# Expert products as plain fp32 in four column groups of the array, on weights that are not split

## What is computed

```python
def expert_choice_ffn(h, w_router, w_gate, w_up, w_down):
    t = h.reshape(bsz * seq, d)
    cap = CAPACITY_FACTOR * n_tok // N_EXPERTS
    probs = jax.nn.softmax(t.astype(jnp.float32) @ w_router.astype(jnp.float32), axis=-1)
    aff, idx = lax.top_k(probs.T, cap)
    xe = t[idx]
    hid = jax.nn.silu(jnp.einsum("ecd,edf->ecf", xe, w_gate)) * jnp.einsum("ecd,edf->ecf", xe, w_up)
    ye = jnp.einsum("ecf,efd->ecd", hid, w_down) * aff[..., None].astype(h.dtype)
    out = jnp.zeros_like(t).at[idx.reshape(-1)].add(ye.reshape(-1, d))
```

## Time and profile before

| | us |
|---|---|
| median of 3 runs | 2584.41 (2583.43 to 2584.87) |
| the profiled execution, its own time | 2584.44 |
| its span in the trace | 2582.5 |
| TensorE busy | 2542.2 |
| VectorE busy | 2194.6 |
| ScalarE busy | 1543.3 |
| first product of the experts starts | 1053.57 |
| last product starts | 2564.90 |

### The profile page before, as it was taken

One profiled execution on the slowest core, in us unless ns is written; L12 is line 12 of the kernel. 1 busy time (PEld: TensorE's weight loads), 2 busy tenths in 40 slices (PEclk: granted clock), 3 DMA queues, 4 the chain that ended last, 5 costly groups with the idle time before them and its releaser, 6 DMA issues.

```text
span 2582.5 us, 34113 instructions
## 1 busy us (share of the span) xinstructions
PE 2542.2 (98%) x13271; PEld 1978.6 (77%) x13271; DVE 2194.6 (85%) x2470; ACT 1543.3 (60%) x1781; POOL 349.4 (14%) x419
## 2 busy tenths in 40 slices
PE   9899999999999999999999999999999999999997
PEld 9788899989988888676767767767667677667765
DVE  6989888988887344899999999999999999999997
ACT  5344444444435122577777777777777777777775
POOL 0322332233321000100000000000000000000002
PEclk9899999999999999899999999999999999999999
DMA  4233223422347343999999999999999999999996
GB/s 174 65 107 125 95 95 104 132 95 95 132 135 261 134 149 119 390 392 378 373 374 378 382 367 384 372 378 370 378 381 374 371 382 371 377 378 371 373 379 244
DMA packets 72303, 705.99 MB, mean 273 GB/s; under 512 B 9840, under 2 KB 14064, under 8 KB 49616
## 3 DMA queue, kind: packets, MB, share of 16 engines
q1 hardware_dynamic: 49232, 628.92, 62.8%
q0 software_dynamic: 14272, 56.60, 7.1%
q10 hardware_dynamic: 8640, 18.29, 1.9%
HBM read 669.72 MB, written 34.06 MB: 273 GB/s over the span
## 4 chain that ended last, share of the span: by engine, by line
PE 95%; DVE 2%; DMA 1%; issue 1%; ACT 1%; POOL 0%; ACTq 0%; DVEq 0%; POOLq 0%
PE p_gu L2462 38%; PE p_y L2493 19%; PE pp L1087 17%; PE pp L1295 5%; PE pp L1131 5%; PE pp L1324 2%; PE pdg L1182 2%; PE p_h L2474 1%; PE off_banks L1165 1%; PE ptr L1149 1%; PE pp L1405 1%; DMA h<-rows 1%; PE off_banks L1179 1%; PE off_banks L1177 1%; PE ptr L1341 0%
## 5 line engine op out<-in xcount | busy, mean ns | idle before, releaser
L2344 DVE TENSOR_TENSOR wl<-raw,wh 128x2048 fp32r<-128x2048 f32 x528 | 1194.2, 2290 | 116.7 <-ACT wh L2241 106.4
L2241 ACT ACTIVATE wh<-raw 128x2048 fp32r<-128x2048 f32 x528 | 990.8, 1911 | 230.5 <-PE p_y L2493 223.1
L2462 PE MATMUL p_gu<-wh,xh 128*96 128x512 f32 x1408 | 566.4, 402 | 1.6 <-DVE xl L2358 1.5
L2462 PE MATMUL p_gu<-wh,xl 128*96 128x512 f32 x1408 | 555.7, 395 | 0.0
L2462 PE MATMUL p_gu<-wl,xh 128*96 128x512 f32 x1408 | 553.7, 393 | 0.0
L2462 PEld LDWEIGHTS p_gu<-wl,xh 128*96 128x96 f32 x1408 | 227.5, 162 | 100.2 <-issue 0.3
L2462 PEld LDWEIGHTS p_gu<-wh,xh 128*96 128x96 f32 x1408 | 227.6, 162 | 90.6 <-DVE wl L2344 2.3
L1087 PE MATMUL pp<-h_hi,wx_hi 128*128 128x256 f32 (+1 forms) x832 | 296.0, 356 | 0.5 <-ACT fo L673 0.5
L2462 PEld LDWEIGHTS p_gu<-wh,xl 128*96 128x96 f32 x1408 | 227.5, 162 | 83.3 <-issue 0.2
L1087 PE MATMUL pp<-h_hi,wx_lo 128*128 128x256 f32 (+1 forms) x832 | 282.7, 340 | 0.0
L1087 PE MATMUL pp<-h_lo,wx_hi 128*128 128x256 f32 (+1 forms) x832 | 281.6, 339 | 0.0
(11 more groups left out here) (283 smaller groups left out, 3798.0 us busy)
## 6 DMA issues: line engine op xcount, KB each, us to landing
raw<-in_w_e SPq DMA_DIRECT2D x176, 3072.0 KB, 10.9
w_raw<-in_w_x SPq DMA_DIRECT2D x48, 512.0 KB, 3.5
dec<-acs POOLq DMA_DIRECT2D x48, 512.0 KB, 4.8
w_raw<-in_w_g SPq DMA_DIRECT2D x24, 512.0 KB, 3.5
g_tab<-gx POOLq DMA_DIRECT2D x8, 1152.0 KB, 6.0
w_raw<-in_w_s SPq DMA_DIRECT2D x16, 512.0 KB, 3.8
gx<-fo ACTq DMA_DIRECT2D x16, 384.0 KB, 3.1
ys<-yt ACTq DMA_DIRECT2D x14, 384.0 KB, 2.7
```

The lines of the kernel that those rows point to most:

```text
L2241: act.activation(wh[:, n % 2, at:at + hi - lo], raw[:, n % RAW, lo:hi], ACT.Copy).then_inc(s_wh, 1)
L2344: dve.tensor_tensor(wl[:, n % 2, to], raw[:, n % RAW, lo:hi], wh[:, n % 2, to].bitcast(F32), ALU.subtract).then_inc(s_wl, 1)
L2462: mm = pe.matmul(p_gu[n % 2][0:SLOTS, 0:w], xx[:, side, k * SLOTS:(k + 1) * SLOTS], ww[:, n % 2, k * w:(k + 1) * w], start=(k == 0 and i = ...
```

## The change

- **No split.** `wh`, `wl`, `xl`, `hid_lo` and the instructions that write them are gone. TensorE multiplies the raw fp32 weights with fp32 tokens.
- **Column groups.** The 96 tokens are three groups of 32. A job is one group of tokens by one tile of 128 hidden columns: 8 products of 256 columns (gate and up) with a 128 x 32 stationary operand. There are 3 x 22 x 16 = 1056 jobs. Four of them make a round, one in each quarter of the array's columns, with the result on partitions 0, 32, 64 and 96 of `p_gu`. There are 264 rounds, and every three rounds finish four tiles.
- **Down.** For each tile, the first 768 columns of the result go as 2 x 3 products of 384 columns to partitions 0 to 95 of `p_y`, and the last 256 as 3 products to partition 96, in `p_y` and in a new bank `p_z`.
- **Transposes.** Each round has one `turn` of 128 x 128 on the whole array, between the two halves of the next round's `gate_up`.
- **ScalarE and VectorE** keep the silu, on 128 x 128, the copies of the turned hidden values and tokens, and the results.
- **Loads.** `raw` has seven slots, and a load waits for `down` of the unit seven before. Unit 0 is asked for where it was. Units 1 and 2 are asked for after GpSimd has issued the prompt's gather, 3 and 4 after the mixer's stores have landed, 5 and 6 after `chosen`.
- **The end.** Squares and norms lie one per round in the last six rounds.

The core of the diff (of functions that are replaced as a whole, mostly the new lines):

```diff
-UNITS = (2,) * 11
-NU = len(UNITS)
-RAW = 3
-UT = max(UNITS)
-TURN_AT = 5
-UW = UT * P * (2 * KD + KD)
+UT = 2
+NU = FT // UT
+EARLY_RAW = 3
+RAW = 7
+TW = P * (2 * KD + KD)
+UW = UT * TW
+QUADS = 4
+GROUPS = SLOTS // 32
+JOBS = GROUPS * FT * E
+ROUNDS = JOBS // QUADS
+HELD = 4
...
                     sp.wait_ge(s_o, NT)
                     load_unit(sp, A, e_raw, s_eraw, 0, 0)
-                    load_unit(sp, A, e_raw, s_eraw, 0, 1)
                 sp.wait_ge(s_h, t + 1)
                 sp.dma_start(h2[t * P:(t + 1) * P, 0:D], hh[:, t % 2, :]).then_inc(s_h2[t % 2], 16)
             sp.wait_ge(s_pr, 2)
             sp.dma_start(probs_of(NTP, NT), prob[:, NTP:NT]).then_inc(m_pr2, 16)
-            load_unit(sp, A, e_raw, s_eraw, 0, 2)
...
-        wh = a.sb("wh", [P, 2, UW], F32R)
-        wl = a.sb("wl", [P, 2, UW], F32R)
+        more = a.sb("more", [P, RAW - EARLY_RAW, UW])
+        raw = [*raw, more[:, 2], more[:, 3], more[:, 0], more[:, 1]]
...
-        hl = a.sb("hid_lo", [P, 2, UT * SLOTS], F32R)
+        xT = a.sb("xT", [P, 2, KD * SLOTS])
+        a.sb("lists", [P, KD * SLOTS * 2])
+        tg = a.sb("tg", [P, 2, P])
+        hid = a.sb("hid", [P, 2, P])
+        hT = a.sb("hidT", [P, HELD, P])
...
+        def job(t, g):
+            return GROUPS * t + g
+        def turned_by(t):
+            return job(t, GROUPS - 1) // QUADS
+        def downs(r):
+            return [t for t in range(FT * E) if turned_by(t) == r]
+        def tiles_read(r):
+            return (QUADS * r + QUADS - 1) // GROUPS + 1
+        def result_at(e):
+            return turned_by(FT * (e + 1) - 1) + 1
+        def tokens_at(e):
+            return turned_by(FT * (e - 1) + FT // 2)
...
+        y_first = [p_y[:, b * 512:b * 512 + 3 * P] for b in range(2)]
+        y_last = [t[quad(3), 0:2 * P] for t in (p_y[:, 0:512], p_y[:, 512:1024], p_z)]
+        LAST_AT = 6 * P
...
-            def load(e, u):
-                n = NU * e + u
-                sp.wait_ge(s_wh, 3 * n + 3)
-                sp.wait_ge(s_wl, 3 * n + 3)
-                load_unit(sp, A, raw, s_raw, e, u)
-
+            def load(n):
+
+                sp.wait_ge(s_dn, UT * (n - RAW) + UT)
+                load_unit(sp, A, raw, s_raw, n // NU, n % NU)
+
+            sp.wait_ge(s_go, 2)
+            load_unit(sp, A, raw, s_raw, 0, 1)
+            load_unit(sp, A, raw, s_raw, 0, 2)
             listed(sp)
-            for u in range(RAW, NU):
-                load(0, u)
+            load_unit(sp, A, raw, s_raw, 0, 3)
+            load_unit(sp, A, raw, s_raw, 0, 4)
+            sp.wait_ge(s_xt, 1)
+            load_unit(sp, A, raw, s_raw, 0, 5)
+            load_unit(sp, A, raw, s_raw, 0, 6)
             sp.dma_start(nfin[:], A["norm_final"].partition_broadcast(P)).then_inc(f_n, 16)
             sp.dma_start(idx_o[:], idx[CAPS[0]:SLOTS, E - 1:E]).then_inc(f_io, 16)
-            for e in range(1, E):
-                for u in range(NU):
-                    load(e, u)
-            sp.wait_ge(s_wh, 3 * NU * E + 3)
-            sp.wait_ge(s_wl, 3 * NU * E + 3)
+            for n in range(RAW, NU * E):
+                load(n)
+            sp.wait_ge(s_dn, UT * (NU * E - RAW) + UT)
             sp.wait_ge(s_sc, 16 * (E - 1))
...
             pool.indirect_dma_start(xe[0:CAPS[0], :], None, h2[0:SEQS[0], :],
                                     bass.IndirectOffsetOnAxis(ap=idx_g[0:CAPS[0], 0:1], axis=0)).then_inc(s_g, 16)
+            pool.sem_inc(s_go, 1)
             listed(pool)
...
-                act.activation(wh[:, n % 2, at:at + hi - lo], raw[:, n % RAW, lo:hi], ACT.Copy).then_inc(s_wh, 1)
...
+            def gated(r):
+                act.wait_ge(s_gu, r + 1)
+                if r >= 2:
+                    act.wait_ge(s_hid, r - 1)
+                act.activation(tg[:, r % 2, :], p_gu[r % 2][:, 0:P], ACT.Tanh, scale=0.5).then_inc(s_tg, 1)
+            def hidden(r):
+                act.wait_ge(s_t, r + 1)
+                if r >= HELD:
+                    act.wait_ge(s_dn, tiles_read(r - HELD))
+                act.activation(hT[:, r % HELD, :], p_h[:, 0:P], ACT.Copy).then_inc(s_hT, 1)
+            def tokens(e):
                 act.wait_ge(s_xt, e + 2)
+                act.activation(tiles(xT[:, e % 2, :]), turned, ACT.Copy).then_inc(s_xc, 1)
...
+                for g in range(GROUPS):
+                    ins = act.activation(ye[quad(g), LAST_AT:D], y_last[g], ACT.Copy, scale=aff[quad(g), e:e + 1])
+                ins.then_inc(s_ye, 1)
...
-                dve.tensor_tensor(wl[:, n % 2, to], raw[:, n % RAW, lo:hi], wh[:, n % 2, to].bitcast(F32),
-                                  ALU.subtract).then_inc(s_wl, 1)
...
+                dve.tensor_scalar(first_cols(ye[:, 0:LAST_AT]), first_cols(p_y[0:SLOTS, :])[:, :, 0:3 * P],
+                                  aff[:, e:e + 1], None, ALU.mult).then_inc(s_ye, 1)
...
+            def weights(t):
+                return raw[t // UT % RAW][:, t % UT * TW:(t % UT + 1) * TW]
+            def gate_up(r, half):
+                placed = [divmod(QUADS * r + q, GROUPS) for q in range(QUADS)]
                 if half == 0:
+                    if r >= 2:
+                        pe.wait_ge(s_hid, r - 1)
+                    for t, g in placed:
+                        if g == 0 and t % UT == 0:
+                            pe.wait_ge(s_raw[t // UT % RAW], 16 * (t // UT // RAW + 1))
+                        if g == 0 and t % FT == 0:
+                            pe.wait_ge(s_xc, t // FT + 2)
                 for k in range(half * KD // 2, (half + 1) * KD // 2):
+                    for q, (t, g) in enumerate(placed):
+                        mm = pe.matmul(p_gu[r % 2][quad(q), 0:2 * P], xT[:, t // FT % 2, k * SLOTS + 32 * g:k * SLOTS + 32 * (g + 1)],
+                                       weights(t)[:, k * 2 * P:(k + 1) * 2 * P], start=(k == 0), stop=(k == KD - 1))
                 if half == 1:
                     mm.then_inc(s_gu, 1)
+            def turn(r):
+                pe.wait_ge(s_hid, r + 1)
+                if r >= 1:
+                    pe.wait_ge(s_hT, r)
+                pe.transpose(p_h[:, 0:P], hid[:, r % 2, :], ident[:]).then_inc(s_t, 1)
+            def hidden(t, g):
+                r, q = divmod(job(t, g), QUADS)
+                return hT[:, r % HELD, quad(q)]
+            def added(t, b):
+                f = t % FT
+                w = weights(t)[:, 2 * KD * P:TW]
+                pe.wait_ge(s_hT, turned_by(t) + 1)
+                for g in range(GROUPS):
+                    pe.matmul(y_first[b][quad(g), :], hidden(t, g), w[:, b * 3 * P:(b + 1) * 3 * P],
+                              start=(f == 0), stop=(f == FT - 1))
+                for g in ((0, 1), (2,))[b]:
+                    mm = pe.matmul(y_last[g], hidden(t, g), w[:, LAST_AT:D], start=(f == 0), stop=(f == FT - 1))
                 return mm
+            def down(t):
+                if t and t % FT == 0:
+                    pe.wait_ge(s_ye, 2 * (t // FT))
+                added(t, 0)
+                added(t, 1).then_inc(s_dn, 1)
...
+            def closing():
+                r, t = ROUNDS - 1, FT * E
+                turn(r - 1)
+                gate_up(r, 1)
+                added(t - 3, 0)
+                turn(r)
+                added(t - 3, 1).then_inc(s_dn, 1)
+                down(t - 2)
+                for b in range(2):
+                    added(t - 1, b).then_inc(f_y, 1)
...
+            gate_up(0, 0)
+            gate_up(0, 1)
+            for r in range(ROUNDS - 1):
+                gate_up(r + 1, 0)
+                if r == ROUNDS - 2:
+                    closing()
+                else:
+                    turn(r)
+                    gate_up(r + 1, 1)
+                    for t in downs(r):
+                        down(t)
+                    for e in range(1, E):
+                        if r == tokens_at(e) - 1:
+                            tokens(e)
```

More of the change, by code:

```diff
@@ L2382, in hidden_low @@
-            def hidden_low(e, u):
-                n, w = NU * e + u, UNITS[u] * SLOTS
-                dve.wait_ge(s_hh, n + 1)
-                dve.tensor_tensor(hl[:, n % 2, 0:w], p_h[n % 2][:, 0:w], hh[:, n % 2, 0:w].bitcast(F32),
-                                  ALU.subtract).then_inc(s_hl, 1)
-            def expert(e, side, last):
-                for u in range(1, NU - 2 if last else NU):
-                    unit(e, u, following(e, u))
-                    if u == TURN_AT and not last:
-                        tokens(e + 1, 1 - side)
-                if last:
-                    closing(e)
-                else:
-                    unit(e + 1, 0, following(e + 1, 0))
@@ new lines, in _ @@
+            dve.wait_ge(s_xt, 2)
+            dve.tensor_copy(tiles(xT[:, 0, :])[:, :, lo:hi], at).then_inc(s_xc, 1)
+            for r in range(ROUNDS):
+                gated(r)
+                for e in range(E - 1):
+                    if r == result_at(e):
+                        result(e)
+                if r >= NORMS_AT:
```

(37 more changed lines are left out.)

320 lines of the change are left out of this document (66 added, 254 removed).

## The result

The changed kernel takes 2562.8 us (median of 4 runs, 2560.9 to 2567.0), the kernel before on the same chip 2583.9 (2583.4 to 2584.9). The ratio is 0.992, 95% interval 0.990 to 0.994. It is faster by 0.8%, where 0.4% was forecast. The execution profiled took 2560.9 us, its span is 2559.1.

The account below looks back on a forecast made before the run. TensorE alone was taken as the bound. Start 1052.5, clock 1.0 and products 1499.6 end at 2553.1, 12.0 us earlier; a tail 1.5 longer leaves 10.5 off 2584.44, so 2574, range 2560 to 2585 (chance 0.50).

Parts of the forecast that it names:

- `gate_up`, 0.2155 a record in each group: Expert products: 16 records a group at 0.2155 us, 3.448 us a round, 910.3 us over 264 rounds.
- `down`, 1.293 a tile: Down products: the fourth group's 6 records of 256 columns at 0.2155 us set a tile; 455.1 us over 352 tiles.
- `turn`, 0.45: Whole-array transpose between group products: 0.33 us for changing form plus 0.11 for the transpose; 264 times, 118.8 us.
- The 0.33 for changing the form: TensorE around a turn: going from column groups to the whole array and back once costs 0.33 us.
- The start, 1052.5: First expert product starts at about 1052.5 us, for 1053.57 before; an earlier gather can win at most 0.31 us.
- 1 us for a lower clock: First expert products: 1 us added for the clock at the lower level.
- The tail, +1.5: After the last product: about 1.5 us longer, the last norm standing ahead of both sums, five short instructions, on VectorE.
- Free change of form: Rival at the turns: the change is nearly free inside a stream, 97 us less, 2477, loads holding about 2500; chance 0.14.
- A dearer turn: Rival at the 264 turns: each costs more and the kernel gets slower, 2590 to 2605, at most 2661; chance 0.20.
- Operands slower in a long run: Rival in group products: four streams of different weights get operands slower than in a burst; 1% costs 14 us, 2588; chance 0.11.
- The start: unit 1: Rival at the start: unit 1 comes late because gather and two loads share the queue; five us at most, 2579; chance 0.03.
- The fourth rival: In `down`: records of different groups end in program order, fourth group 0.2 us behind per run; 53 us, 2627; chance 0.02.

Follow-up runs that it names:

- run 1: Against the changed kernel, each turn is four plain fp32 products in column groups with the identity instead of one whole-array transpose; 2518.5 us.
- run 2: Against the changed kernel, each turn issues its transpose twice, one behind the other, into the same place; 2591.6 us.
- run 3: Against the changed kernel, each turn is a plain fp32 product of the whole array with the identity (two records) instead of a transpose; 2606.3 us.
- run 4: Against the changed kernel, units 1 and 2 are asked for when the prompt's gather has landed, not when it has been issued; 2563.9 us.
- run 6: Against the changed kernel, from unit 7 on a load waits for `down` of the unit four before, not seven, except the last ten; 2570.1 us.

## Why the prediction was right, and what was off in it

Faster was right, and so was the mechanism; the gain was 0.8% and not 0.4%. Against the execution profiled (own time 2560.9) the forecast of 2574 was 13.1 us too long. The forecast's gain of 10.5 us is a small difference of large sums, and by its own working a turn of 0.49 us instead of 0.45 would have eaten all of it. That the turn was off by as much as that, but to the other side, is luck for the word "faster". By its steps:

- **`gate_up`, 0.2155 a record in each group:** right. A second half with the first sweep after the turn takes 1.75 us, in run 1 it takes 1.73, and 8 x 0.2155 is 1.724. The price, taken between the halfway value of the earlier trace rows and that of the earlier trace rows, held over 1.5 ms.
- **`down`, 1.293 a tile:** measured 1.29.
- **`turn`, 0.45:** the step that was mis-sized. It measured 0.40, and 264 x 0.05 = 13.2 us is as much as the whole miss. The 0.33 for changing the form was taken from the earlier trace rows, where the whole product has weights of the plain kind. Runs 2 and 3 show that a transpose, whose weight load is shorter, costs 0.05 us less there. The forecast knew the transpose's own 0.11 and added it, but not that its load is shorter as well.
- **The start, 1052.5:** measured 1054.29, later by 1.8. The step that failed is "it can't win more than those 0.31 us", which allowed for no loss: the gather shares the queue with two loads that are asked for as it is sent off, and it was waited for 1.30 us where the forecast had no wait left. The rest is the mixer, 0.35 later in this execution, and 0.14 of small parts.
- **1 us for a lower clock:** didn't come; the granted clock was 1.00 over 1056 to 1100. It came in executions in which TensorE had waited for more than 2 us (0.60 behind a wait of 2.33 us for a unit in run 4, 0.54 to 0.73 behind the gather in runs 1, 3 and 6).
- **The tail, +1.5:** measured 0.0; the trace ends 17.6 us after the last product's start in both. The delay that was forecast is there: ScalarE's square comes 3.49 us after the last product's start instead of 1.52, because a norm of 1.28 us and five short sums stand ahead. But three things give it back. GpSimd begins 1.30 us after the square and not 1.65, its two instructions for the norm's factor take 0.85 us to VectorE's start instead of 1.94, and the scatter of the result no longer stands behind stores of other rows, for which it waited before: it starts 0.97 us after the norm's end and not 1.53. The forecast followed the chain one step and not to its end. The changed kernel, then the one before:

```profile
2544.98 1.06 ACT L2298 ACTIVATE ye<-xg 96x1024 f32<-96x1024 f32 x1 [5.00 <-DVE xg L2331]
2547.13 1.41 DVE L2358 SCALAR_TENSOR_TENSOR xg<-xg,rstdf,nfin 96x512 f32<-96x512 f32 x2 [2.18 <-POOL rstdf L2236]
2549.51 1.02 POOL L2242 DMA_INDIRECT out<-xg,idx_g  x1 [2.42 <-issue]
...
2572.95 1.02 POOL L2224 DMA_INDIRECT out<-xg,idx_g  x1 [2.97 <-DMA out<-raw]
```

Summed: start +1.8, clock -1.0, products 1487.5 to their last column for 1499.6, -12.1, tail -1.5, in all -12.8 for the 13.1 found. Start, clock and tail, each off by 1 to 2 us, cancel to -0.7, and that too is luck.

**The rivals.** Free change of form: no, 0.29 of 0.40 us is the change, as run 1 shows by taking it away. A dearer turn: no. Operands slower in a long run: no; 0.2155 stayed even at 413 GB/s. The start: unit 1 was in time.

**The fourth rival, ends in program order.** In the rows of two rounds above, the fourth group's records in `down` start at 1304.47 and, third one, at 1304.90, which is two passes of 0.215 after its first; the other three groups start at 1304.45 and 1304.77, 0.32 apart. So the fourth group is through its first product at 1304.90, when its next one starts, and the three products of 384 columns that were issued ahead of it are through theirs only at 1305.09. Each group runs at its own pace, and a tile takes the 1.29 us of the longest group. The Trainium skill, "TensorE: Matmul & The Clock Gate", section "Part 3: Packing small matmuls", says that matmuls start and end strictly in program order; between column groups the rows here bear that out for the starts of the products and not for their ends.

## What to carry to other kernels

When a product is put into column groups, put what stands between the products into groups as well, a transpose by the identity too: here one whole transpose between group products cost 0.40 us where its own work is 0.11, and four group products that do the same cost 0.22, 44 us over 264 places. Price a change of form from a row with the same kind of operation on both sides, weight load included. And "behind" a DMA in the program is not behind it in the queue: look at when both are asked for.

## What the runs showed of the hardware that was not expected

- **The change between groups and the whole array** costs 0.29 us in and out (0.40 a turn less 0.109 for the transpose itself), though no other engine is waited for. The 0.055 us of the next point are part of it.
- **A transpose's weight load** leaves 0.055 us uncovered where a plain fp32 product's leaves about 0.10: 0.33 less 0.27 in the rows of run 2, and the 0.05 of run 3 on top of it. Its record is 0.138 us long, that of the plain product 0.188.
- **Four groups beside each other keep full pace** for 1.5 ms, and while transfers run at 413 GB/s: 1.73 us for 8 records of 256 columns in run 1, 0.216 each.
- **GpSimd beside VectorE.** A GpSimd instruction on one number per partition took 0.19 us in the changed kernel's end, with VectorE idle, and 1.28 in the kernel before, where VectorE's norm of 1.28 us runs over the same time. In the kernel before, by time:

```profile
2568.02 1.28 DVE L2434 SCALAR_TENSOR_TENSOR raw<-raw,rstdf,nfin 128x1024 f32<-128x1024 f32 x1 [0.44 <-POOL rstdf L2214]
2568.07 1.28 POOL L2217 TENSOR_SCALAR ssqf<-ssqf 96x1 f32<-96x1 f32 x1
```

And in the changed kernel:

```profile
2546.28 0.19 POOL L2235 TENSOR_SCALAR ssqf<-ssqf 96x1 f32<-96x1 f32 x1 [5.34 <-ACT ye L2298]
```

The one row is not alone. Seven such instructions stand at the end of the kernel before. Five took 0.95 to 1.45 us, each beside a norm or a subtraction of VectorE on `raw` and each ending within 0.06 us of it; two took 0.19, one (at 2556.77) as VectorE fell idle and one (at 2565.84) beside VectorE's sums out of `p_y`. In the changed kernel VectorE is idle beside all seven, and all take 0.18 or 0.19. No experiment was made on it.
